# Second layer's norm ahead of the feed-forward: where its first weight panel is split, and where the square root's table is loaded

## What is computed

```python
x_lat = x_lat + gt1 * y_out                      # y_out = y @ w_out, the matmuls of the panels "wo"
h = rms_norm(x_lat, g_mlp[l]) * (1 + sc2) + sh2  # "n2.1" in the kernel
x_lat = x_lat + gt2 * (square(relu(h @ w_ff1[l])) @ w_ff2[l])   # panels "ff1", "ff2"

def rms_norm(x, g):
    return x * rsqrt(mean(x * x, axis=-1) + EPS) * g
```

## The kernel before

| place | panel | buffer | its fetch waits for |
|---|---|---|---|
| 154 | wo 3 | t_28 | second half of wo 0 split |
| 155 | ff1 0 | t_29 | second half of wo 1 split |
| 156 | ada 53 | t_27 | second half of wo 2 split |
| 157 | ada 54 | t_28 | second half of wo 3 split |
| 158 | ada 55 | t_29 | second half of ff1 0 split |
| 159 | ff1 1 | t_27 | ada 53 multiplied |
| 160 | ff1 2 | t_28 | ada 54 multiplied |
| 161 | ff1 3 | t_29 | ada 55 multiplied |

## Time and profile before

### The profile page before, as it was taken

One profiled execution on the slowest core, in us unless ns is written; L12 is line 12 of the kernel. 1 busy time (PEld: TensorE's weight loads), 2 busy tenths in 40 slices (PEclk: granted clock), 3 DMA queues, 4 the chain that ended last, 5 costly groups with the idle time before them and its releaser, 6 DMA issues. The chain is left out here.

```text
span 2072.2 us, 31551 instructions
## 1 busy us (share of the span) xinstructions
PE 2017.6 (97%) x12882; PEld 1677.5 (81%) x12882; DVE 1128.8 (54%) x2231; ACT 906.8 (44%) x1632; POOL 63.3 (3%) x85
## 2 busy tenths in 40 slices
PE   5999999999999999999999999999999999999998
PEld 3888767779777777788789899997877678888877
DVE  4437662446433343466665777642465444445886
ACT  4446762335423131255664554443334332233685
POOL 0000000001000000100000000000000000000100
PEclk8999999999999999999999999999999999999999
DMA  8222015533344444443126554444211243222311
GB/s 305 97 92 97 16 49 191 198 132 123 144 183 186 179 163 164 184 161 117 36 77 229 223 192 173 182 168 183 102 42 61 82 168 137 89 99 97 122 62 42
DMA packets 47104, 277.15 MB, mean 134 GB/s; under 512 B 4464, under 2 KB 12784, under 8 KB 16752
## 3 DMA queue, kind: packets, MB, share of 16 engines
q1 hardware_dynamic: 42080, 266.94, 34.9%
q10 hardware_dynamic: 4736, 7.34, 1.1%
q0 software_dynamic: 144, 0.85, 0.1%
HBM read 273.01 MB, written 2.10 MB: 133 GB/s over the span
## 5 line engine op out<-in xcount | busy, mean ns | idle before, releaser
L579 PE MATMUL ps<-t 128*128 128x512 f32 (+1 forms) x2184 | 757.1, 347 | 4.6 <-DVE t L1799 4.3
L581 PE MATMUL ps<-t 128*128 128x512 f32 (+1 forms) x2184 | 750.2, 344 | 0.0
L580 PE MATMUL ps<-t 128*128 128x512 f32 (+1 forms) x2184 | 750.2, 343 | 0.0
L1799 DVE TENSOR_TENSOR t<-t 128x1024 fp32r<-128x1024 f32 (+2 forms) x370 | 414.2, 1160 | 260.9 <-ACT t L1215 260.2
L579 PEld LDWEIGHTS ps<-t 128*128 128x128 f32 x2184 | 412.4, 189 | 69.0 <-issue 8.4
L1215 ACT ACTIVATE t<-t 128x1024 fp32r<-128x1024 f32 (+2 forms) x378 | 359.6, 1000 | 220.2 <-PE ps L581 155.5
L581 PEld LDWEIGHTS ps<-t 128*128 128x128 f32 x2184 | 412.3, 189 | 50.9
L580 PEld LDWEIGHTS ps<-t 128*128 128x128 f32 x2184 | 412.4, 189 | 49.9 <-issue 0.7
L1785 DVE TENSOR_TENSOR t<-t 128x512 f32<-128x512 f32 (+10 forms) x621 | 231.7, 393 | 206.4 <-ACT t L1315 73.2
L1315 ACT ACTIVATE t<-ps 128x512 f32<-128x512 f32 (+1 forms) x244 | 115.6, 492 | 348.0 <-PE ps L581 236.8
L1794 DVE SCALAR_TENSOR_TENSOR t<-ps,t 128x256 f32<-128x256 f32 (+2 forms) x176 | 83.1, 496 | 180.0 <-PE ps L581 159.7
(11 more groups left out here) (167 smaller groups left out, 2070.4 us busy)
## 6 DMA issues: line engine op xcount, KB each, us to landing
t<-in_panels SPq DMA_DIRECT2D x236, 1024.0 KB, 4.8
t<-in_panels SPq DMA_DIRECT2D x19, 512.0 KB, 3.5
t<-in_panels SPq DMA_DIRECT2D x6, 768.0 KB, 4.1
t<-in_window ACTq DMA_DIRECT2D x4, 768.0 KB, 4.3
t<-in_ctxT SPq DMA_DIRECT2D x1, 1024.0 KB, 14.1
t<-in_xT SPq DMA_DIRECT2D x1, 1024.0 KB, 16.3
t<-in_ctxT ACTq DMA_DIRECT2D x1, 1024.0 KB, 5.7
t<-in_xT ACTq DMA_DIRECT2D x1, 1024.0 KB, 8.2
```

Of the source, the lines that this page charges most:

```text
L579: e.matmul(o, hi[:, k, w], xh[:, c0:c1], start=k == 0, stop=False)
L580: e.matmul(o, hi[:, k, w], xl[:, c0:c1], start=False, stop=False)
L581: t = e.matmul(o, lo[:, k, w], xh[:, c0:c1], start=False, stop=k == p.nk - 1)
L1799: e.tensor_tensor(p.half(wlo[p.buf], a), p.half(raw[p.slot], a), p.half(whi[p.buf], a).bitcast(F32), ALU.subtract).then_inc(*up(ve, ("lo", ...
```

## The change

Three things are moved, all in the norm of the second layer ahead of the feed-forward (`n2.1`).

- DVE no longer splits ff1 0 ahead of the last two residuals (`begin(wo 3)` is left out for it there). The first half is split behind the sum of squares of block 7, ahead of the reciprocal; the second half amid the features, behind the scaling of blocks 2 and 3 and ahead of the low part of block 2. ACT's half of the split stays where it was.
- ACT's root of the dummy column, and with it the table load, stands ahead of the squares of blocks 6 and 7 and no longer behind them.
- Nothing is moved on PE, POOL or SP; no instruction is added or taken away.

```diff
@@ ACT, rms and turn
-                if x == "c" or s == "n2.1":
+                if x == "c":
                     own()
                     e.activation(root[:, :], epst[:, :], ACT.Sqrt).then_inc(*up(se))
...
             def turn(s, kind, l, vb, parts, p):
 
+                if s == "n2.1":
+                    own()
+                    e.activation(root[:, :], epst[:, :], ACT.Sqrt).then_inc(*up(se))
                 for j in range(2):
                     stat(s, 6 + j, parts[0])
@@ DVE, turn
-            def turn(s, kind, l, vs, vb, parts, last, pair=None):
+            def turn(s, kind, l, vs, vb, parts, last, pair=None, held=None):
...
                 for j in range(2):
                     last(j, parts[0])
                     stat(s, 6 + j, parts[0])
+                if held:
+                    lo(held, 0)
+                    nxt[0] = held.i + 1
...
-                modulate(s, "l", kind, l, vs, vb)
+                modulate(s, "l", kind, l, vs, vb, [(lambda: None, lambda: None), (lambda: lo(held, 1), lambda: None)] if held else ())
@@ DVE, first_layer
-                begin(at["wo", l, 3])
+                if not last:
+                    begin(at["wo", l, 3])
                 rows_out()
                 fold("b", l, 4, f"gmlp{l}")
                 turn(s, "b", l, 4, 3, parts, lambda j, x: residual(s, 6 + j, split_key(("wo", l, 6 + j), x), "b", l, 2, x),
-                     None if last else at["ff1", l, 1])
+                     None if last else at["ff1", l, 1], at["ff1", l, 0] if last else None)
```

## The result

| | before | after |
|---|---|---|
| median | 2074.78 us (2074.05 to 2076.56, 5 runs) | 2082.64 us (2081.47 to 2083.37, 5 runs) |
| ratio, 95% interval | | 1.0038 (1.0027 to 1.0048) |
| profiled execution, its span | 2074.14, 2072.2 us | 2081.47, 2079.6 us |

A forecast was written before the change was run, and what follows sets the result against it. PE is busy 97% of the span, so only its idle stretches count. ff1 1 starting at 1184.0 instead of 1176.85 adds 7.2 us to 2074.14, giving 2081.3; the median lies 0.6 above, 2081.9 us, range 2079.2 to 2084.0.

The forecast's parts named there:

- part 5: SP's fetch of ada 55 waits for the split's second half, leaves 9.25 us later; ff1 1 starts 7.2 us later; 75%.
- A: Rival: ada 55 isn't bound to the moved half, so the kernel gets faster, 2073.8 us, at best 2072.3; 5%.
- B: Rival: ada 55 is bound, but its transfer lands at 1174.3 and the clock is not low: +4.4, 2079.2 us; 9%.
- C: Rival: three fetches share the wires, ada 55 takes 8.2 us to land: +3 on the sum, 2084.9 us and more; 6%.
- parts 1, 2: In the norm, split moved from ahead of the last residuals, table load ahead of the squares: reciprocal 1.0 us earlier.
- part 3: Split's first half, 1.2 us, behind the sums, ends 0.1 us ahead of the reciprocal's input: cost nothing, uncovered up to 1.2.
- part 4: Split's second half amid the features ends at 1169.5; low part 2 starts behind it, costing the features 0.2 us.
- part 2: Table load ahead of the squares on ACT: square 6 waits 1.6 us, the root starts at 1163.6 instead of 1164.59.
- The clock: After PE resumes at 1174.4, full clock returns after 3.8 to 7.0 us; ff1 0 loses 0.9 to 2.3, taken 1.5.
- The total: ff1 1 starts 7.2 us later: profiled execution 2081.3 us, median 2081.9 us.
- Rival D: Split's first half misses its cover, the reciprocal waits, the feature path is 1.2 us later: 2083.1 us; 5%.

## Why the prediction was right

The forecast (part 5) was the case that came, and the other cases are told apart by the runs: A is out, as the fetch did not leave near 1160 but at 1171.4; B and C are out by the rows of the profile after (PE had half its clock behind the wait, and the first of the three fetches landed 4.7 us after it left). Step by step, counted from T0 (the prediction's times less 1160.85, those of after less 1162.24):

| step | predicted | measured |
|---|---|---|
| reciprocal starts (parts 1, 2) | 3.25 | 3.2 |
| time between the end of the first half and the reciprocal (part 3) | 0.1 | 0.28 |
| second half ends (part 4) | 8.65 | 9.1 |
| fetch leaves | 8.7 | 9.1 |
| landing | 4.7 to 5.6 | 4.7 |
| ada 55 starts, lasts | 13.55 to 14.45, 1.93 | 14.0, 1.94 |
| ff1 0 lasts | 7.3 | 6.4 |
| ff1 1 starts | 23.15 | 22.3 |

- **Parts 1 and 2** held: the squares, the sum and the root came where the sum of durations put them, and the 1.0 us won on the activation's path is real. The run with ada 55 behind ff1 0 shows it on PE, too: ff1 0 at 6.8 in place of 7.8. But part 2 gave the table load a share in it, and by the run with the table back it has none.
- **Part 4** was short by 0.5 us. I took 1.2 us for the second half, from halves that ran while POOL had nothing to do. Amid the features POOL works beside it, and it took 1.75 us (below).
- **Part 5**, the wait of SP, held in its place, its length and in what is queued behind it. The run with the late fetch alone shows that it is the cause.
- **The clock** was mis-sized. I let the low level last 3.8 to 7.0 us after work was resumed, and it lasted 3.1: at 1176.25 us PE starts, and from 1179.3 the full clock is granted. ff1 0 lost 0.6 us by it (6.4 against 5.8), less than the 0.9 to 2.3 of the forecast.

```profile
1176.20:1178.10 1.90, 1.85 (x16) 0.68 (x16) 0.00 (x0) 0.00 (x0) 0.00 (x0) 0.50 0.99 414
1178.10:1179.30 1.20, 1.20 (x9) 1.19 (x6) 0.00 (x0) 0.95 (x2) 0.00 (x0) 0.50 1.04 437
1179.30:1184.50 5.20, 5.20 (x45) 5.20 (x44) 2.36 (x2) 1.56 (x3) 0.00 (x0) 0.99 0.91 312
```

  With the table back, in the same place and order, it lasted 5.4 us and ff1 0 took 7.4 us. So the 7.3 was one of the values that this stretch can take, not a constant.
- **The total** agrees better than its parts, and that is luck: the profiled execution took 2081.47 us where the sum gave 2081.3, but the stretch grew by 6.3 and not by 7.2 us, and 1.4 us were lost ahead of T0, where nothing differs between the kernels (above). The median of after lies 7.9 us above that of before, with an interval of 5.6 to 10.0 that holds the 6.3; what makes up the rest of the 7.9 is open. What the change itself costs is best read from the yardsticks, 6.3 us in this execution; the late fetch alone gives 6.4, and 7.2 is what comes with the longer low clock (23.2 - 16.0).
- **Rival D** did not come about: DVE was through with the first half 0.28 us ahead of the reciprocal and stood idle, and what the reciprocal waited for was ACT's root. The cover of part 3 was there, with a little more to spare than I had worked out.

## What to carry to other kernels

A split, a copy or any other step that empties a ring buffer is also what lets the next fetch leave: before moving it later, look up which fetch waits for it, what stands behind that fetch in the same queue, and where in the matmul queue the first panel of them is due. It is cheap to move such a step as long as the fetch, the landing and the short work on that panel still end ahead of the next wait of the matmul engine; here 0.6 us later was free and 4.7 us later cost 1.5, in kernels whose reciprocal came 0.7 and 0.2 us earlier besides. And count the clock with a wait: in each of these profiles PE had half its clock for 3.1 to 5.8 us, directly or soon behind its longest wait in the stretch (2.0 to 11.4 us). That makes a new wait cost more than its length (2.6 us more, with ada 55 behind ff1 0), but here there was such a stretch before as well, and the loss was no more than the added idle time. Compare two kernels by the stretch that the change touches, as falls of the clock elsewhere differ from run to run by more than a small change is worth.

## What the runs showed of the hardware that was not expected

**DVE's split beside POOL.** The same subtraction of 128x1024 took 1.22 us for the first half and 1.75 us for the second. The DVE rows, then POOL's at the same time:

```profile
1163.96 1.22 DVE L1802 TENSOR_TENSOR t<-t 128x1024 fp32r<-128x1024 f32 x1
...
1169.59 1.75 DVE L1802 TENSOR_TENSOR t<-t 128x1024 fp32r<-128x1024 f32 x1
1171.26 1.73 DVE L1797 SCALAR_TENSOR_TENSOR t<-t 128x256 fp32r<-128x256 f32 x3
```
```profile
1170.69 1.23 POOL L2486 TENSOR_TENSOR t<-t 128x256 fp32r<-128x256 f32 x1 [0.44 <-ACT t L1275]
...
1175.47 0.72 POOL L2486 TENSOR_TENSOR t<-t 128x256 fp32r<-128x256 f32 x1 [0.44 <-ACT t L1275]
```

POOL's subtraction of 128x256 took 1.23 us beside it, and 0.85 at the same block in the kernel before; the run with ada 55 behind ff1 0 repeats both (1.76 and 1.25). The Trainium skill says in its GPSIMD Engine Reference, Specifications, that the SBUF interfaces are shared with VectorE, with contention for DVE instructions with two SBUF inputs; the split is one of these, and these rows agree, with 0.5 us on DVE and 0.4 on POOL. POOL's first low part, of which the last two thirds ran beside the split, took 1.02 us, and 1.03 in the kernel before, where DVE's scalings ran beside it; so the split is not the only instruction of DVE that goes with a longer one of POOL. No run here tells this contention apart from another reason why both get slower together.

**A group of fetches.** The first of three fetches issued 0.4 and 0.5 us apart lands as if it were alone (4.7 or 4.8 us in five kernels), and the third takes 10.1 to 10.3 us, more than the 8.2 us that were the longest in the earlier trace rows. The second took 6.8 to 6.9 us in four of them and 8.1 in the fifth.
